# A transformer block on one core: places of w_out given back row by row, four loads ahead of the pass number, own positions for expert 0, tiles at multiples of 256

## The reference, cut to what matters

```python
x = x + merged @ w_out[l]
h2 = rms_norm(x, norm_ffn[l])
# hier_moe: 4 groups of 8 experts; the best group of a token, and in it its best two experts
p_group = softmax(xt @ w_rg + b_rg); group = argmax(p_group)
top_p, top_i = top_k(softmax((xt @ w_re + b_re) of that group), 2)
weights = p_group_top * top_p / sum(top_p)
y = sum over a token's two experts e of weight * (silu(xb @ w_g[e]) * (xb @ w_u[e])) @ w_d[e]
x = x + y
```

## Time and profile before

| | us |
|---|---|
| median of three timed runs | 711.92 |
| the profiled execution | 712.9 |
| its span in the trace | 711.1 |
| PE busy in the span | 587.2 |
| DVE busy | 302.8 |
| ACT busy | 189.7 |

### The profile page before, as it was taken

The page is one execution under the profiler, slowest core; times in us unless marked ns, Lnnn a source line. Parts: engine busy times, 40 slices in busy tenths (PEclk is TensorE's granted clock), DMA queues, the critical chain, the costliest instruction groups (busy, mean ns, idle before and its releaser), DMA issues.

```text
span 711.1 us, 15452 instructions
## 1 busy us (share of the span) xinstructions
PE 587.2 (83%) x6636; PEld 410.9 (58%) x6636; DVE 302.8 (43%) x626; ACT 189.7 (27%) x332; POOL 29.6 (4%) x56
## 2 busy tenths in 40 slices
PE   8999999999999999996875767776678656887584
PEld 5787899999999885553432333333334333443342
DVE  6475976985474945442222222122312222111412
ACT  4493355473535434110111001010011100110111
POOL 8003000000000020000000000000000000000000
PEclk9999999999999999998798788797877988687969
DMA  8995546536579699999999999999999999999993
GB/s 253 349 328 187 163 137 203 175 121 213 175 274 420 234 395 369 427 425 428 425 427 425 426 429 427 426 427 427 425 425 428 427 427 427 424 426 427 423 417 146
DMA packets 39619, 247.73 MB, mean 348 GB/s; under 512 B 4360, under 2 KB 6496, under 8 KB 25472
## 3 DMA queue, kind: packets, MB, share of 16 engines
q1 hardware_dynamic: 38096, 245.44, 85.6%
q0 software_dynamic: 912, 1.25, 1.0%
q10 hardware_dynamic: 544, 0.06, 0.1%
HBM read 245.67 MB, written 1.06 MB: 347 GB/s over the span
## 4 chain that ended last, share of the span: by engine, by line
PE 50%; DMA 44%; SPq 1%; another core or an unknown queue 1%; DVE 1%; issue 1%; ACT 0%; ACTq 0%; DVEq 0%
DMA wide<-in_w_expert_up 38%; PE ps L1366 8%; PE ps L1029 6%; PE ps L1030 6%; PE ps L1031 6%; DMA wide<-in_w_expert_down 3%; PE ps L1401 3%; PE ps L1002 3%; PE ps L1004 3%; PE ps L1003 3%; PE ps L1325 2%; DMA ring<-in_w_in 2%; PE ps L1413 1%; PE ps L1381 1%; SPq L526 1%
## 5 line engine op out<-in xcount | busy, mean ns | idle before, releaser
L1366 PE MATMUL ps<-wide,xe 128*32 128x256 f32 x2048 | 162.1, 470 | 109.3 <-DMA wide<-in_w_expert_up 109.3
L1366 PEld LDWEIGHTS ps<-wide,xe 128*32 128x32 f32 x2048 | 75.9, 131 | 176.9 <-issue 132.1
L1882 DVE TENSOR_TENSOR xe<-ps,g_ffn 128x256 f32<-128x256 f32 x32 | 13.6, 425 | 258.4 <-PE ps L1334 258.4
L1486 DVE TENSOR_TENSOR ring_lo<-ring,w_hi 128x1024 fp32r<-128x1024 f32 x76 | 92.0, 1228 | 46.2 <-ACT w_hi L721 45.7
L721 ACT ACTIVATE w_hi<-ring 128x1024 fp32r<-128x1024 f32 x76 | 79.0, 1058 | 58.8 <-PE ps L1031 35.3
L1029 PE MATMUL ps<-hT_hi,w_hi 128*128 128x256 f32 x320 | 89.4, 279 | 0.2 <-DVE hT_lo L1498 0.2
L1030 PE MATMUL ps<-hT_lo,w_hi 128*128 128x256 f32 x320 | 88.4, 276 | 0.0
L1031 PE MATMUL ps<-hT_hi,ring_lo 128*128 128x256 f32 x320 | 88.4, 276 | 0.0
L925 ACT ACTIVATE he<-ps 128x128 f32<-128x128 f32 x32 | 8.9, 278 | 207.7 <-PE ps L1381 204.7
L1401 PE MATMUL ps<-wide,he 128*32 128x256 f32 x1024 | 62.5, 382 | 1.9 <-DMA wide<-in_w_expert_down 1.8
L1029 PEld LDWEIGHTS ps<-hT_hi,w_hi 128*128 128x128 f32 x320 | 60.1, 188 | 0.7 <-issue 0.7
(11 more groups left out here) (276 smaller groups left out, 785.9 us busy)
## 6 DMA issues: line engine op xcount, KB each, us to landing
wide<-in_w_expert_gate SPq DMA_DIRECT2D x27, 2048.0 KB, 45.6
wide<-in_w_expert_up SPq DMA_DIRECT2D x27, 2048.0 KB, 48.2
wide<-in_w_expert_down SPq DMA_DIRECT2D x27, 2048.0 KB, 41.1
ring<-in_w_in SPq DMA_DIRECT2D x8, 2048.0 KB, 16.1
ring<-in_w_merge_gate SPq DMA_DIRECT2D x6, 2048.0 KB, 9.6
wide<-in_w_expert_gate SPq DMA_DIRECT2D x10, 1024.0 KB, 13.2
wide<-in_w_expert_up SPq DMA_DIRECT2D x10, 1024.0 KB, 10.6
wide<-in_w_expert_down SPq DMA_DIRECT2D x9, 1024.0 KB, 11.8
```

Source lines behind the costliest of these rows:

```text
L1366: ins = t_.matmul(ps[q * WIN:(q + 1) * WIN, b, 0:QW], xe[b][:, k % 2, k // 2, :], w, start=(k == 0), stop=(k == KD - 1))
L1486: v.tensor_tensor(piece(ring_lo, g, c), piece(ring, g, c), by_row(out_hi[g == 19][c]).bitcast(F32), ALU.subtract).then_inc(wpre_lo, 1)
```

## The change

Five edits. (1) Places of w_out are given back earlier: loads 12 and 14 wait for the first four steps k of `out_half` (both halves of the tokens) and no longer for all eight, and are issued ahead of 13 and 15. In a quarter of the second half, the products with the low part for the second half of the tokens are all done first, so that load 16 and load 17 wait for these eight products and no longer for the quarter's (for 17: both quarters') end. (2) Loads 22 to 25, as two transfers of 2 MB, are issued before SP reads the number of passes. (3) Expert 0 gets positions of its own, from a small tile `first` (is a token's choice expert 0) and six products of one column each; the positions of all experts come after its rows have been picked, and with them expert 1's `pick_w`, which stood ahead of expert 0's `xe` before. (4) The eight seeds are spread in another way, all of them ahead of expert 0's rows. (5) Tiles start at multiples of 256 bytes (small ones of 64) in place of 32; the units' addresses, which were 32, 64 or 128 above a multiple of 256, are multiples of 256 afterwards.

The core of the diff:

```diff
-    top = [16512]
+    top = [16640]
+    def fitting(at, size):
+        step = 256 if size >= 1024 else 64
+        return (at + step - 1) // step * step
...
+        first = place("first", [P, TT, TOPK], BF16)
...
                 elif n == 10:
                     sp.wait_ge(branch_done, 12)
-                elif n < 16:
+                elif n in (12, 14):
+                    sp.wait_ge(chunk_done, chunks_before[NPRE - 2] + 1)
+                elif n in (13, 15):
                     sp.wait_ge(proj_done, first_bank[NPRE - 2] + 2)
-                elif n in (16, 18):
+                elif n == 16:
+                    sp.wait_ge(chunk_done, chunks_before[NPRE - 2] + 2)
+                elif n == 18:
                     sp.wait_ge(proj_done, first_bank[NPRE - 2] + 4)
+                elif n == 17:
+                    sp.wait_ge(chunk_done, chunks_before[NPRE - 2] + 3)
                 elif n != 20:
                     sp.wait_ge(proj_done, first_bank[NPRE - 2] + 6)
...
-            for n in [0, 1, 2, 3, 11] + list(range(4, 11)) + [12, 13, 14, 15, 16, 18, 17, 19, 21, 20]:
+            for n in [0, 1, 2, 3, 11] + list(range(4, 11)) + [12, 14, 13, 15, 16, 18, 17, 19, 21, 20]:
                 first_load(n)
+            def next_load(n, done):
+                if n not in paired:
+                    sp.wait_ge(unit_free, done + (UNITS + free_at(n - RING)))
+                elif n % 2 == 0:
+                    sp.wait_ge(unit_free, done + (UNITS + max(free_at(n - RING), free_at(n + 1 - RING))))
+                load_unit(n)
+            for n in range(RING, RING + N_AHEAD):
+                next_load(n, 0)
             sp.wait_ge(route_ready, 1)
             passes = sp.value_load(npass[0:1, 0:1], min_val=1, max_val=MAXWIN)
...
-                for n in range(RING, UNITS):
...
+                for n in range(RING + N_AHEAD, UNITS):
+                    next_load(n, UNITS * p)
...
-            act.wait_ge(slot_ready, 1)
-            s_.activation(flat(tab[:, :, :]), ps[:, 3, 2 * NE:4 * NE], ACT.Copy).then_inc(table_ready, 1)
             rows_copy(0, 0)
+            act.wait_ge(slot_ready, 1)
+            s_.activation(flat(tab[:, :, :]), ps[:, 3, 2 * NE:4 * NE], ACT.Copy).then_inc(table_ready, 1)
...
                 if ks[-1] == KD - 1:
                     ins.then_inc(proj_done, 1)
+                elif tt == TT - 1:
+                    ins.then_inc(chunk_done, 1)
...
+                if tt and ks[0] == 0:
+                    for k in range(KD):
+                        ins = t_.matmul(o, merged_hi[:, k, rows], wl[k], start=(k == 0), stop=False)
+                    ins.then_inc(chunk_done, 1)
...
-            out_quarter(1, 1, range(0, 4))
+            out_quarter(1, 1, range(0, 2))
...
+            seed(0, 0)
             route(1, range(6, KD), 6)
-            seed(0, 0)
+            seed(0, 2)
+            seed(1, 0)
+            seed(1, 2)
             seed(0, 1)
...
+            pe.wait_ge(assign_ready, 1)
+            for k in range(TOPK):
+                first_spot(tri_bf[:, :], 0, k, 0, start=(k == 0), stop=False)
+                first_spot(ones_bf[:, :], 0, k, 1, start=False, stop=False)
+                ins = first_spot(tri_bf[:, :], 1, k, 1, start=False, stop=(k == TOPK - 1))
             ins.then_inc(pos_mm, 1)
+            seed(0, 3)
+            seed(1, 1)
+            seed(1, 3).then_inc(seeded, 1)
...
             pick_rows(0, 0)
+            all_spots()
             turn_rows(0, 0)
-            seed(1, 1).then_inc(seeded, 1)
...
+            v.tensor_tensor(first[:, :, :], iota_f[:, 0:1].unsqueeze(1).broadcast_to([P, TT, TOPK]), ie8[:, :, 0:TOPK],
+                            ALU.is_equal).then_inc(assign_ready, 1)
+            dve.wait_ge(assign_ready, 1)
+            link(v.tensor_tensor(stat[:, 44:46].unsqueeze(2), first[:, :, 0:1], first[:, :, 1:2], ALU.add))
...
             dve.sem_inc(same_ready, 1)
+            rows_in(0, 0)
+            slots()
             dve.wait_ge(table_ready, 1)
             choose(0, 1)
-            rows_in(0, 0)
```

More of the change, by code:

```diff
@@ L71 @@
 N_SMALL = 15
+N_AHEAD = 4
 CHUNK_T = 2
@@ L195, in hybrid_block @@
         npass = place("npass", [1, 1], I32)
-        region = top[0]
+        region = fitting(top[0], 1024)
         def here(name, shape, dt):
-            nonlocal_at = here_at[0]
-            here_at[0] += (int(np.prod(shape[1:])) * mybir.dt.size(dt) + 31) // 32 * 32
-            return place(name, shape, dt, at=nonlocal_at)
+            size = int(np.prod(shape[1:])) * mybir.dt.size(dt)
+            off = fitting(here_at[0], size)
+            here_at[0] = off + size
+            return place(name, shape, dt, at=off)
         here_at = [region]
-        sig0_at = here_at[0]
+        sig0_at = here_at[0] = fitting(here_at[0], 1024)
         sig0 = here("sig0", [P, KD, T], F32)
@@ L582, in _ @@
                         load_unit(n)
-                for n in range(RING, UNITS):
-                    if n not in paired:
-                        sp.wait_ge(unit_free, UNITS * p + (UNITS + free_at(n - RING)))
-                    elif n % 2 == 0:
-                        sp.wait_ge(unit_free, UNITS * p + (UNITS + max(free_at(n - RING), free_at(n + 1 - RING))))
-                    load_unit(n)
+                    for n in range(RING, RING + N_AHEAD):
+                        next_load(n, UNITS * p)
+                for n in range(RING + N_AHEAD, UNITS):
+                    next_load(n, UNITS * p)
             for tt in range(TT):
@@ L1230, in out_quarter @@
                     wh = out_hi[1][c][:, QW * (k % 4):QW * (k % 4 + 1)]
-                    wl = ring_lo[19 % PRE_RING][:, UNIT * q + QW * k:UNIT * q + QW * (k + 1)]
-                    t_.matmul(o, merged_hi[:, k, rows], wh, start=(k == 0), stop=False)
-                    t_.matmul(o, merged_hi[:, k, rows], wl, start=False, stop=False)
+                    t_.matmul(o, merged_hi[:, k, rows], wh, start=(tt == 0 and k == 0), stop=False)
+                    if tt == 0:
+                        t_.matmul(o, merged_hi[:, k, rows], wl[k], start=False, stop=False)
                     ins = t_.matmul(o, merged_lo[:, k, rows], wh, start=False, stop=(k == KD - 1))
@@ L1243, in turn_x1, with seed @@
                 ins.then_inc(x1_turned, 1)
-            def seed(tt, half):
-                for q in (2 * half, 2 * half + 1):
-                    ins = t_.matmul(bank(4 + q, 2)[:, tt, :], ident[:, :], x_tok[:, tt, QW * q:QW * (q + 1)],
-                                    start=(tt == 0), stop=False, skip_group_check=True)
-                return ins
+            def seed(tt, q):
+                return t_.matmul(bank(4 + q, 2)[:, tt, :], ident[:, :], x_tok[:, tt, QW * q:QW * (q + 1)],
+                                 start=(tt == 0), stop=False, skip_group_check=True)
             def route(tt, ks, copied):
@@ L1299, in spots, with first_spot, all_spots @@
                                  skip_group_check=True, **flags)
-            for tt in range(TT):
-                pe.wait_ge(assign_ready, 2)
-                for k in range(TOPK):
-                    spots(ones_bf[:, :], below[:, tt, k, :], 0, 3, start=(tt == 0 and k == 0), stop=False)
-                    spots(tri_bf[:, :], eh[:, tt, k, :], tt, 1, start=False, stop=False)
-                    if tt == 0:
-                        spots(ones_bf[:, :], eh[:, 0, k, :], 1, 1, start=False, stop=False)
-                    ins = spots(ones_bf[:, :], eh[:, tt, k, :], 3, 1, start=False, stop=(tt == 1 and k == 1))
-            ins.then_inc(pos_mm, 1)
+            def first_spot(lhsT, tt, k, at, **flags):
+                return t_.matmul(ps[:, 2, at:at + 1], lhsT, first[:, tt, k:k + 1], skip_group_check=True, **flags)
+            pe.wait_ge(assign_ready, 1)
[3 more added lines that the diff above has]
+                ins = first_spot(tri_bf[:, :], 1, k, 1, start=False, stop=(k == TOPK - 1))
+            ins.then_inc(pos_mm, 1)
+            seed(0, 3)
+            seed(1, 1)
+            seed(1, 3).then_inc(seeded, 1)
+            def all_spots():
+                for tt in range(TT):
+                    pe.wait_ge(assign_ready, 3)
+                    for k in range(TOPK):
+                        spots(ones_bf[:, :], below[:, tt, k, :], 0, 3, start=(tt == 0 and k == 0), stop=False)
+                        spots(tri_bf[:, :], eh[:, tt, k, :], tt, 1, start=False, stop=False)
+                        if tt == 0:
+                            spots(ones_bf[:, :], eh[:, 0, k, :], 1, 1, start=False, stop=False)
+                        ins = spots(ones_bf[:, :], eh[:, tt, k, :], 3, 1, start=False, stop=(tt == 1 and k == 1))
+                ins.then_inc(pos_mm, 1)
             def rows(values, ready, b):
@@ L1335, in turn_rows @@
                 ins.then_inc(rows_turned, 1)
-            seed(1, 0)
             pe.wait_ge(xn0_ready, 1)
@@ L1845, in _ @@
             v.tensor_tensor(eh[:, :, :, :], every, chosen, ALU.is_equal).then_inc(assign_ready, 1)
```

(5 more changed lines are left out.)

63 lines of the change are left out of this document (30 added, 33 removed).

## The result

The changed kernel is slower: median 714.62 us of five runs (713.66 to 715.81) beside 711.92 us of five runs of the kernel before on the same chip (711.28 to 712.20), a ratio of 1.0034 with a 95% interval of 1.0022 to 1.0046, so 1.6 to 3.3 us more. 709.7 was forecast, with 711.9 as the upper end. The profiled executions differ by less, 713.66 and 712.9 us: that of before is 1.0 above its median, that of after the lowest of its five.

A forecast was written before the change was run, and what follows sets the result against it. Transfer of expert weights bounds the kernel from some 245 us, PE's dense products before. 712.9 profiled less 2.2 (edits 1 to 4; edit 5 taken as 0) gives 710.7; the median lies 1.0 below: 709.7, range 704.5 to 711.9.

The forecast's parts named there:

- I take 0: Stream of expert weights, 245 to 693 us: tile places differing in offset do not differ in rate, so 0 us.
- none of the moments of the dense part moves: Quarters of the dense part: each piece keeps its number of PE products, so its moments stay as before.
- Rival (a): Stream of weights: aligned places touch 64 pieces, not 65; rate up 1.5%, 6.6 us less, 703 us in all; chance 0.15.
- the 3 us: Stream from 245 to 693 us: slices spread by 0.7%, bounding the effect of new addresses either way.
- The account of the average engine: Average DMA engine from 245 us: 6.77 us lost in dips before, 5.95 after, a gain of 0.8 us.
- the new dips: DMA queue dry before loads 17, 19, 20, 22, 26: 1.3, 0.7, 1.15, 2.4 and 0.4 us lost.
- the old ones: DMA dips before the change at 245 to 252, 263 to 268, 271 to 278 us: 3.57, 1.08, 2.12 us.
- the laggard: Last DMA engine to finish, which sets the end: lost 8.2 us over loads 10 to 20; gain taken as 2.2 us.
- the reading of the pass number: SP's read, now behind load 24: hidden by 7 us of queue; without that cover it cost 0.8 us before load 22.
- (b): No new dips: the last engine's 8.2 us are all idle and covered; up to 6.8 us go, 706; chance 0.10.
- (d): Slower: expert 1's rows come late behind DVE's longer chain, delaying loads 26, 28, 30; up to 713.5 us; chance 0.08.
- (c): The gain is eaten by dips as for the average engine: 0.8 us gained, 711.1 us; chance 0.17.

The follow-up runs named there:

- e1: Kernel before with only the new memory map (tiles at multiples of 256 bytes), order of work unchanged: 715.81 us beside 712.76, ratio 1.0042.
- e3: Whole block left out, only TensorE products of constant tiles, 64 pairs of operand offsets in 64-byte steps: 256-column products start every 113.5 to 120.2 ns.
- e7: Whole block left out, only products of constant tiles, 64 offset pairs in steps of 32 bytes: all start every 114 to 120.2 ns.
- e8: Changed kernel with every tile 128 bytes higher: 717.48 us beside 712.59 of the kernel before, ratio 1.0064.
- e9: Changed kernel with every tile 64 bytes higher: 718.18 us in one run.
- e2: Changed kernel on the memory map of the kernel before: 711.49 us beside 712.76 of the kernel before, ratio 0.9991.
- e6: e2 with no load issued ahead of the pass number (loads 22 to 25 wait): 712.95 us beside 712.48 of the kernel before, ratio 1.0008.
- e5: Changed kernel with units kept at multiples of 256 bytes, TensorE's dense operands back at old offsets: 708.32 us beside 712.48 of the kernel before, ratio 0.9944.
- e10: Whole block left out, only products of constant tiles, 48 of one offset pair after different pairs: that of the kernel before starts every 113.5 or 117.8 ns.
- e4: Changed kernel with hT_hi, hT_lo and merged_hi 192 bytes lower, 64 past a multiple of 256: 713.84 us beside 712.48 of the kernel before, ratio 1.0026.

## Why the prediction was wrong

**The step that failed** is edit 5, "I take 0", and with it the sentence that none of the moments of the dense part moves. I looked at the new addresses as targets of transfers alone. They are TensorE's operands as well: in the dense part both operands of each product came to the same offset modulo 256, which showed no fast rhythm for products of 256 columns in any run (e1, e3, e7, e8, e9), and `out_half` starts 6.3 us later. The Trainium skill (TensorE: Matmul & The Clock Gate, Step-by-step: what each phase is for) says that the loading of the next weights takes no read bandwidth from the running product, as the two have a port each. In e3, with no other engine at work, the interval between products still goes from 113.5 to 120 ns by the offset of one operand to the other. Whether the two reads collide or something else does is not shown.

**Rival (a) was half right.** The stream is faster, 429 for 426 GB/s, 54.30 to 53.94 us a ring: 0.7% and not 1.5%, so 0.36 x 8.1 rings = 2.9 us of the 6.6. That is the 3 us which I had worked out as a bound and then set to 0. My reason for 0, that three offsets ran alike, did not speak of the fourth: the mix of 32, 64 and 128, 64 alone and 128 alone are alike, and only 0 differs (e8, e9). The Trainium skill's rule (DMA: Bandwidth & Descriptors, How a descriptor splits into AXI transactions) names just this boundary, though for the bytes that a transfer fetches, and here it is the written side that moved. The loss that it gives by unused bytes, an estimate, would be half as large at 64 as at 128, and it was the same.

**Edits 1 to 4: the moments right, the sum too large.** Loads 12 and 14 were forecast for 241.2, load 17 for 259.3, 20 for 268.5, 22 for 273.0, and 26 for 0.4 earlier than 283.57; in e2 they went out at 241.14, 259.36, 268.27, 272.95 and 283.09. The first gate_up, forecast for 271.0, started at 270.93. The account of the average engine holds too. By mean landings the new dips at loads 17, 19, 20, 22 and 26 are 1.1, 0.4, 1.1, 2.4 and 0.9 us, together 5.9 where 5.95 were forecast; the old ones come to some 7.3 by the same measure, where the windows gave 6.77. The mis-sized term is the laggard. I took 2.2 us, as if the last engine had its own extra work and kept what it won; it wins the same 1.2 as all the others (e2). From load 10 to load 20 the last engine takes 26.8 us there, 33.0 before, so most of what it lost in the kernel before was idle time. Its lead of 5.6 us went at loads 22, 24 and 26, where it is 2.9 us behind the average again (before 2.8). Load 26 goes out only 0.48 us earlier than before, as its place is freed by PE's work on expert 1. That the reading of the pass number would cost 0.8 us without its cover was too little: in e6 place 4 lands 1.5 later than in e2, in part because DVE's chain now makes this number 1.1 us later (at 273.56, before at 272.45).

**Rivals (b) and (d)** fell: there are new dips, and expert 1's rows were in time (in e2 `xe` starts at 276.70, before at 276.62). For these four edits (c), with 0.8 us, came nearest. In the changed kernel PE goes from its last products for the tables at once to expert 1's gate_up (283.35 and 1.06 us, then 284.33), and load 26 goes out no later than by the general shift.

**The sum put right:** 6.3 (dense) - 2.9 (stream) - 1.3 (edits 1 to 4) = 2.1 us more; measured 2.4 (1.6 to 3.3). And without the first term -4.2, as e5 measured. The terms may not add up as exactly as that: with the new addresses in both, the changed kernel's place 4 lands only 0.65 us ahead of e1's (297.42 for 298.07). One reading of the prediction was loose and touched no sum: 423 to 429 GB/s hold to the thirty-eighth slice, and the last but one has 417.

## What to carry to other kernels

An address is read by every engine that touches it, so a change of a memory map is a change of all of them: go through who reads each tile, and compare the starts of the products in a stretch where the code did not change. Give the targets of a DMA-bound stream multiples of 256 bytes, but keep the two operands of TensorE's back-to-back products of 256 columns at different offsets modulo 256, here 64 and 128; at 512 columns equal offsets cost nothing (e3). And when an earlier issue fills a dip in a queue, the next late issue takes it back: of 3.6 us filled, 1.2 to 1.3 were kept, and none without the load that follows.

## What was not expected of the hardware

- Two rhythms for one pair of tiles, 113 and 118 ns, kept for dozens of products (e10, and the 48 in the kernel before and in e4). What ran before has a part in which it is, but the pair just before does not decide it.
- 0.7% of the stream's rate by the offset of its targets in SBUF, all or nothing at 256 bytes: 53.94 us a ring at 0, 54.30 to 54.34 at 64 and 128.
- In e10 TensorE waited 2.3 us for VectorE, after a stretch at a granted clock of 1.00; the clock of the 3 us that followed was 0.50, the lower level of 1.2 GHz, and products started every 213 ns. Behind the run's two other such waits it fell to 0.50 as well (94 to 96 us: 0.50; 113.6 to 116: 0.55):

```profile
57.00:60.00 3.00, 3.00 (x28) 3.00 (x28) 0.00 (x0) 0.00 (x0) 0.00 (x0) 1.00 0.02 5
60.40:62.90 2.50, 0.23 (x2) 0.02 (x1) 1.76 (x1) 0.00 (x0) 0.00 (x0) 0.95 0.00 0
62.90:64.00 1.10, 1.06 (x5) 1.06 (x6) 0.00 (x0) 0.00 (x0) 0.00 (x0) 0.50 0.00 0
```
